# Weaving the MLA projection into the stick-breaking and MLA attention pipelines

## The reference

```
p = rmsnorm(x) @ w_in                      # 1024 -> 3*512 (q, k, v) + 384 + 256 + 32
o_sb  = stick-breaking attention, 8 heads of 64:
        z = q k^T / 8; A = exp(log_sigmoid(z) + sum over s<j<t of log_sigmoid(-z)), strictly causal; A v
q     = rmsnorm(c_q)  @ w_uq  -> 8 heads of 64 + 32 (the 32 get a rotary embedding)
k, v  = rmsnorm(c_kv) @ w_ukv -> 8 heads of 64 + 64, plus one rotary key of 32 shared by the heads
o_mla = softmax(q k^T / sqrt(96), causal) v
x = x + concat(rmsnorm(o_sb), rmsnorm(o_mla)) @ w_out
x = x + (silu(gate) * val) @ w_down,  gate, val = causal depthwise conv of rmsnorm(x) @ w_up
return rmsnorm(x)
```

## Time and profile before

| | |
|---|---|
| median of 2 runs | 3560.66 us (3554.89 to 3566.42) |
| the profiled execution's own time | 3548.83 us |
| its span on the slowest core (core 7) | 3546.7 us |
| spans of the 8 cores | 3519.6 to 3546.7 us, granted TensorE clock 0.940 to 0.947 of full speed |
| PE busy | 2507.5 us, 71% |
| ACT busy | 2076.0 us, 59% |
| DVE busy | 1425.7 us, 40% |
| POOL busy | 882.0 us, 25% |

### The profile page before, as it was taken

One profiled execution on the slowest core, in us unless ns is written; L12 is line 12 of the kernel. 1 busy time (PEld: TensorE's weight loads), 2 busy tenths in 40 slices (PEclk: granted clock), 3 DMA queues, 4 the chain that ended last, 5 costly groups with the idle time before them and its releaser, 6 DMA issues.

```text
span 3546.7 us, 57426 instructions; the slowest of 8 cores (3519.6 to 3546.7 us)
## 1 busy us (share of the span) xinstructions
PE 2507.5 (71%) x15344; PEld 1186.8 (33%) x15344; DVE 1425.7 (40%) x3146; ACT 2076.0 (59%) x4420; POOL 882.0 (25%) x1477
## 2 busy tenths in 40 slices
PE   4876666667656878788838766666676568787877
PEld 2432333234322333333324333232343233333333
DVE  3432222230314566666544322222303145666675
ACT  2458888867653444444234588888676544444442
POOL 2012222232332222222220122222323322222221
PEclk9999999999988999999969999999999889999999
DMA  5100000000039656565451000000000396566563
GB/s 112 48 14 1 1 1 1 1 1 1 1 78 136 90 95 85 95 92 82 60 120 48 13 1 1 1 1 1 1 1 1 75 142 99 88 91 92 87 86 63
DMA packets 211365, 178.48 MB, mean 50 GB/s; under 512 B 6000, under 2 KB 187248, under 8 KB 211056
## 3 DMA queue, kind: packets, MB, share of 16 engines
q0 software_dynamic: 195072, 119.29, 26.4%
q1 hardware_dynamic: 15984, 55.53, 4.8%
HBM read 277.30 MB, written 16.78 MB: 83 GB/s over the span
## 4 chain that ended last, share of the span: by engine, by line
PE 40%; ACT 22%; DVE 14%; issue 14%; POOL 5%; DMA 4%; ACTq 1%; another core or an unknown queue 1%; DVEq 1%; POOLq 0%; SPq 0%
PE pb L1027 9%; ACT arena L649 7%; PE pb L895 4%; ACT arena L795 4%; DVE arena L923 4%; PE pb L897 4%; DVE arena L926 4%; PE pb L634 3%; ACT arena L614 3%; PE pb L988 3%; PE pb L785 3%; PE pb L433 2%; PE pb L595 2%; ACT arena L913 2%; PE pb L636 2%
## 5 line engine op out<-in xcount | busy, mean ns | idle before, releaser
L641 DVE TENSOR_TENSOR arena<-arena 128x512 bf16<-128x512 bf16 (+3 forms) x576 | 226.7, 400 | 783.9 <-PE pb L595 447.6
L634 PE MATMUL pb<-arena,cbf_sb 128*128 128x512 bf16 (+3 forms) x640 | 222.2, 347 | 367.8 <-ACT arena L649 148.3
L895 PE MATMUL pb<-arena 128*128 128x512 bf16 x1408 | 346.7, 391 | 166.7 <-DVE arena L926 80.4
L616 ACT ACTIVATE arena<-arena 128x512 bf16<-128x512 f32 (+3 forms) x640 | 362.0, 566 | 108.7 <-POOL arena L652 24.2
L595 PE MATMUL pb<-arena 128*128 128x512 bf16 (+3 forms) x1280 | 411.3, 350 | 11.7 <-issue 4.3
L795 ACT ACTIVATE arena<-pb 128x512 bf16<-128x512 f32 (+3 forms) x640 | 314.7, 531 | 100.1 <-PE pb L822 65.1
L1027 PE MATMUL pb<-arena 128*128 128x512 bf16 x1408 | 324.6, 394 | 59.3 <-ACT arena L954 29.5
L913 ACT ACTIVATE arena<-pb,cw_sb 128x512 f32<-128x512 f32 x352 | 268.6, 775 | 155.1 <-PE pb L897 154.8
L614 ACT ACTIVATE arena<-pb 128x512 f32<-128x512 f32 (+3 forms) x640 | 336.4, 526 | 2.3 <-PE pb L595 1.9
L897 PE MATMUL pb<-arena 128*128 128x512 bf16 x1408 | 335.9, 382 | 0.0
L649 ACT ACTIVATE arena<-pb 128x512 bf16<-128x512 f32 (+3 forms) x640 | 329.8, 516 | 5.2 <-PE pb L595 3.5
(11 more groups left out here) (127 smaller groups left out, 3772.7 us busy)
## 6 DMA issues: line engine op xcount, KB each, us to landing
arena<-w_up POOLq DMA_DIRECT2D x176, 512.0 KB, 6.7
arena<-x SPq DMA_DIRECT2D x64, 512.0 KB, 4.4
out<-arena SPq DMA_DIRECT2D x32, 512.0 KB, 2.9
arena<-w_down POOLq DMA_DIRECT2D x22, 512.0 KB, 42.5
arena<-w_in POOLq DMA_DIRECT2D x16, 552.0 KB, 24.1
arena<-w_out POOLq DMA_DIRECT2D x16, 256.0 KB, 19.9
arena<-w_uq POOLq DMA_DIRECT2D x6, 192.0 KB, 5.4
arena<-g_mix SPq DMA_DIRECT2D x2, 512.0 KB, 5.5
```

The lines of the kernel that those rows point to most:

```text
L616: op('act', lambda e: e.activation(out=sp_sb[es_][:, 0:n], in_=e_sb[es_][:, 0:n], func=AF.Ln, bias=1.0), reads=[('e', es_)], writes=[('sp' ...
L634: e.matmul(banks[cbk][:, 0:n], lhsT=ntri, rhs=sp_sb[ss_][:, 0:n], start=True, stop=False)
L895: e.matmul(banks[bg][:], lhsT=wup[ws][:, kc, 0:128], rhs=h2T[:, kc, :], start=(kc == 0), stop=(kc == 7))
```

## The change

A second set of Q, K and V arrays is added (`QTm2`, `KTm2`, `Vm2`, "bufB"). Group 0's projection writes into it while SB runs, and group 1's projection writes into the old arrays ("bufA") while group 0's attention reads bufB. The projection is now a generator with 48 micro-steps (A, B, C for each block), of which `weave` issues one after every 6th step of the SB pipeline and after every 3rd of the first MLA attention. Its three banks come from the outputs of the attention: SB now uses banks 4 and 5 for every head, with the projection on 6 and 7; MLA uses 2, 3 and 4 for every head, with the projection on 5, 6 and 7. The barrier between SB and MLA goes. The tiles `qtm`, `ktm` and all of `Vm2` are filled by POOL before the first SB item; the fill of `Vs_flat` with ones stands once, between SB and the first MLA attention.

```diff
+def weave(main_gen, side_gen, every):
+    k = 0
+    for _ in main_gen:
+        k += 1
+        if side_gen is not None and k % every == 0:
+            next(side_gen, None)
+    if side_gen is not None:
+        for _ in side_gen:
+            pass
...
+            QTm2 = A3.take([128, 4, S], BF16)
+            KTm2 = A3.take([128, 4, S], BF16)
+            Vm2_flat = A3.take([128, NB * 260], BF16)
...
-                ob0 = 4 if h % 2 == 0 else 6
+                ob0 = 4
...
-            run_pipeline(sb_items, [(0, sb_s0), (1, sb_s1), (2, sb_s2), (3, sb_s3), (4, sb_s4)])
-            S_.barrier()
...
-                run_pipeline(list(range(NB)), [(0, mp_A), (1, mp_B), (2, mp_C)])
...
+                for tb in range(NB):
+                    step_A(tb)
+                    yield
+                    step_B(tb)
+                    yield
+                    step_C(tb)
+                    yield
...
-                    ob0 = 2 if h % 2 == 0 else 5
+                    ob0 = 2
...
+            for qs_ in range(2):
+                op('pool', lambda e, qs_=qs_: e.memset(qtm[qs_]..., 0.0), writes=[('qtm', qs_)])
+                op('pool', lambda e, qs_=qs_: e.memset(ktm[qs_]..., 0.0), writes=[('ktm', qs_)])
+            op('pool', lambda e: e.memset(Vm2_flat, 1.0), writes=[('Vb', tb) for tb in range(NB)])
+            n_micro = 3 * NB
+            weave(pipeline_gen(sb_items, [(0, sb_s0), (1, sb_s1), (2, sb_s2), (3, sb_s3), (4, sb_s4)]),
+                  mla_proj_gen(0, bufB, 6, 7, 6), max(1, len(sb_items) // (n_micro + 2)))
+            op('pool', lambda e: e.memset(Vs_flat, 1.0), writes=[('V', tb) for tb in range(NB)])
+            items0, stages0 = mla_attn_stages(0, bufB)
+            weave(pipeline_gen(items0, stages0), mla_proj_gen(1, bufA, 5, 6, 7), max(1, len(items0) // (n_micro + 2)))
+            items1, stages1 = mla_attn_stages(1, bufA)
+            run_pipeline(items1, stages1)
```

More of the change, by code:

```diff
@@ L194, in run_pipeline, with pipeline_gen @@
                 fn(items[i])
+def pipeline_gen(items, stages):
+    n = len(items)
+    maxlag = max(l for l, _ in stages)
+    for t in range(n + maxlag):
+        for lag, fn in stages:
+            i = t - lag
+            if 0 <= i < n:
+                fn(items[i])
+        yield
[8 more added lines that the diff above has]
+            pass
 class Arena:
@@ L684, in sb_s4, with mla_proj_gen, step_A @@
                              reads=[bk(bi)], pwrites=[('o', i)])
-            run_pipeline(sb_items, [(0, sb_s0), (1, sb_s1), (2, sb_s2), (3, sb_s3), (4, sb_s4)])
-            S_.barrier()
[L689 to L695, removed]
             MQ = 7
             n_mb = (NB + MQ - 1) // MQ
[L698 to L708, removed]
+            bufA = dict(QT=QT, KT=KT, V=Vs[:, :, 0:260].rearrange("p a (h d) -> p a h d", h=4),
+                        qk=lambda hl: ('QT', hl), kk=lambda hl: ('KT', hl // 2), vk=lambda tb: ('V', tb))
+            bufB = dict(QT=QTm2, KT=KTm2, V=Vm2,
+                        qk=lambda hl: ('QTb', hl), kk=lambda hl: ('KTb', hl), vk=lambda tb: ('Vb', tb))
+            def mla_proj_gen(g, bufs, bq, bkv, bt):
+                QTd, KTd, Vd = bufs['QT'], bufs['KT'], bufs['V']
+                def step_A(tb):
                     def mmq(e):
@@ L748, in mp_B, with step_C @@
                            reads=['kro'], pwrites=[kk_])
-                    op('dve', lambda e: e.tensor_copy(Vm[:, tb, :, 0:64], kvv[:, :, 64:128]), reads=[bk(bkv)], pwrites=[('V', tb)])
-                    S_.wtag(qk_, (g, tb))
-                def mp_C(tb, g=g):
+                    op('dve', lambda e: e.tensor_copy(Vd[:, tb, :, 0:64], kvv[:, :, 64:128]), reads=[bk(bkv)], pwrites=[bufs['vk'](tb)])
+                def step_C(tb):
                     qs = tb % 2
[L754 to L758, removed]
+                    qk_, kk_ = ('qtm', qs), ('ktm', qs)
+                    ptr = banks[bt][:].bitcast(BF16)
                     def trqk(e):
@@ L765, in trqk, with mla_attn_stages @@
                         return ins
[L766 to L770, removed]
-                run_pipeline(list(range(NB)), [(0, mp_A), (1, mp_B), (2, mp_C)])
-                if P3_MODE == 'proj':
-                    S_.enabled = False
+                    op('pe', trqk, reads=[qk_, kk_, 'cbf'], writes=[bk(bt)])
+                    evac(QTd[:, :, tb * 128:(tb + 1) * 128], ptr[:, 0:512].rearrange("p (a b) -> p a b", a=4),
+                         reads=[bk(bt)], pwrites=sorted(set(bufs['qk'](hl) for hl in range(4))))
+                    evac(KTd[:, :, tb * 128:(tb + 1) * 128], ptr[:, 512:1024].rearrange("p (a b) -> p a b", a=4),
+                         reads=[bk(bt)], pwrites=sorted(set(bufs['kk'](hl) for hl in range(4))))
+                for tb in range(NB):
[4 more added lines that the diff above has]
+                    step_C(tb)
+                    yield
+            def mla_attn_stages(g, bufs):
+                QTd, KTd, Vd = bufs['QT'], bufs['KT'], bufs['V']
+                base = mpc[0]
                 m_items = []
```

37 lines of the change are left out of this document (19 added, 18 removed).

## The result

The changed kernel took **1.0141** times the time of the one before (95% interval 1.0110 to 1.0172): about 3603 us against 3553 us, 50 us more. The forecast was 3552 us, in a range of 3480 to 3600; it was added to 3560.66 us, the median of two runs, which lies 7 us above the 3553 us. The profiled execution took 3596.8 us, its span 3595.3 us on core 3.

A forecast was written before the change was run, and what follows sets the result against it. It took ACT to bound SB, and a ring through two score banks the first MLA attention. Per sequence 5.4 + 26 - 38.7 + 36 - 41.9 + 9 = -4.2 us, twice -8.4: 3552 us, range 3480 to 3600.

The forecast's parts named there:

- Parts 1 and 4: Start of SB: POOL's fills, +5.4 us; SB to MLA: a projection stage goes, a fill stays, -38.7 us; per sequence.
- Part 2: Group 0's projection inside SB: ACT's three copies and one evac per block, plus waiting, +26 us per sequence.
- Part 3: One pair of output banks in SB: zeroing waits for both evacs, costing nothing, or up to 0.7 us per head change.
- Part 5: Group 1's projection inside the first MLA attention: 16 blocks at 2.25 us each, +36 us per sequence.
- w: Cost per block of weaving the projection into the first MLA attention: 2.25 us, own range 1.4 to 2.66.
- Part 6: First to second MLA attention: a 42.5 us projection stage goes, zeroing waits 0.6 us more, -41.9 us per sequence.
- Part 7: One set of MLA output banks: zeroing waits 1.5 us at 3 head changes in each group, +9 us per sequence.
- step C stands in PE's queue: First MLA attention: transposes wait for DVE's and POOL's step B, delaying scores and ACT; 3594 us, chance 0.14.
- It hides: First MLA attention: gaps take the woven work whole, at no cost per block; 3480 us, chance 0.18.
- The lock between DVE and GpSimd: Step B: two-input DVE and SBUF-reading GpSimd instructions lock each other out; little weight, 0.3 us per operation, 3650 us.
- the second rival: The rival "step C stands in PE's queue" in the first MLA attention: 3594 us, chance 0.14.

The follow-up runs named there:

- e2_attn_only: Changed kernel with group 0's projection not woven into SB but standing alone before the first MLA attention: 1.0160 of the kernel before, 3603.0 us.
- e4_evac_dve: Changed kernel with both copies of the transposes out of PSUM on DVE, none on ACT: 0.9910 of the kernel before, 3529.8 us.
- e8_filler: Changed kernel plus a 256-column zero-weight matmul behind each product with V of the first MLA attention: no ratio came out.
- e3_kfirst: Changed kernel with POOL's four rotary key copies issued in step A, ahead of ACT's copy: 1.0027 of the kernel before, 3567.2 us.
- e13_kfirst_evac: Changed kernel with POOL's rotary copies issued in step A and both transpose copies on DVE: 0.9856 of the kernel before, 3500.4 us.
- e16_filler512: Changed kernel plus a 512-column zero-weight matmul behind each product with V of the first MLA attention: 1.0094 of the kernel before.
- e6_alt_banks: Changed kernel with the second MLA attention's output banks alternating again between two sets: 1.0078 of the kernel before.
- e9_all_dve: Changed kernel with all projection work of ACT and POOL in steps B and C on DVE: 0.9740 of the kernel before, 3456.0 us.
- e5_kdve: Changed kernel with the rotary key written by one DVE copy in place of POOL's four: no ratio, lowest run 3564.2 us.

## Why the prediction was wrong

**Parts 1 and 4, the start of SB and the handover: right.** Forecast +5.4 and -38.7 us; measured +5.3 (`e2_attn_only`) and -38.8.

**Part 2, the projection inside SB: right in kind, 4.6 us too small.** ACT's own share was right: 22.6 us more busy (forecast 22.7). The term that was too small is the wait before the evac: I had 0.49 + 0.2 us for evac and wait, ACT's idle time there is 0.34 us, and by `e4_evac_dve` the two together cost 0.91 to 0.96 us: (0.22 to 0.27) x 16 = 3.5 to 4.3 us of the 4.6.

**Part 3, one pair of banks in SB: right.** `e2_attn_only` has the single pair, and from the first to the last product with V of SB it takes 506.1 us in the mean, where the kernel before takes 506.3.

**Part 5, the projection inside the first attention: this step failed.** I put w at 2.25 us a block and held 2.66 for its upper end, "if nothing overlaps". From a0, 166.4 - (144.8 - 41.9) - 4.5 = 59.0 us over 16 blocks: w = **3.7 us**, over the bound. The bound was no bound: work put into a ring of in-order engines can cost more than its length, because what queues behind it waits too. The sum of A, B and C looked at PE's and ACT's queues only and left out what POOL's four copies hold up. It shows most in the term for step C: 0.9 to 1.0 us for the transposes, a semaphore step and the evac, where ACT stood 20.9 / 16 = 1.3 us before the evac and then gave it its 0.5. And the sum took PE's durations from stages with a clock of 0.92 to 0.95 as if they would stay.

The 23.0 us divide about so, by estimates. The clock, from `e8_filler`: 13 us gross for 0.78 to 0.93. The order of POOL's copies, from `e3_kfirst`: 17.7 us, of which its own rise of the clock by 0.11 accounts for about 10 at the slope of 94 us, so some 8 directly. Together 21. But the two are not independent, and the slope is only a correlation. The windows would give the clock more: of the 15.5 us between the two stages shown, PE's busy time alone makes 12.7 (111.91 to 99.23). Which share is whose stays open. What the runs do show is the order of the two: taking waits away brought the clock up each time (`e3_kfirst` 0.886, `e4_evac_dve` 0.902, `e13_kfirst_evac` 0.936) and the time with it, while a full clock from fillers (`e16_filler512`, 0.976) left a0 at 160.4 us, the fillers' own price included. So the waits come first, and the lower clock adds to what they cost. No run changed the spacing of the micro-steps or the order of A, B and C among the items, which might remove the same waits.

**Part 6, from the first to the second attention: right**, the stage of 42.5 us went (what stands against it is part 5's).

**Part 7, the changes of heads: right in size.** 1.50 us at the zeroing where I had 1.5. a1 rose by 5.9 us, not 4.5, while the clock fell from 0.954 to 0.917, and `e6_alt_banks` took 7.5 off.

**The rival "step C stands in PE's queue"** had the right price (w = 3.55) by the wrong road: the transposes waited 0.3 us for step B. The queue that mattered was POOL's. Its 3594 us lacked parts 2 and 7's misses. **"It hides"** was far off with this placing of the work, but `e9_all_dve`, with ACT and POOL out of it, comes to w = 0.9 us by the same formula.

**The lock between DVE and GpSimd** was weighed by rows in which POOL ran only copies, and there it doesn't show. Beside POOL's masks, which read two arrays, it does (the first operation of step B's six and the next one on DVE, then POOL):

```profile
838.38 0.38 DVE L749 TENSOR_TENSOR arena<-arena 128x64 f32<-128x64 f32 x1 [5.04 <-ACT arena L744]
838.68 0.21 DVE L750 TENSOR_TENSOR arena<-arena 128x64 f32<-128x64 f32 x1
```

```profile
838.25 0.43 POOL L812 TENSOR_TENSOR arena<-arena,cbf_sb 128x128 bf16<-128x128 bf16 x1 [3.33 <-ACT arena L809]
839.15 1.23 POOL L756 COPY arena<-arena 128x32 bf16<-128x32 bf16 x4 [0.48 <-ACT arena L747]
```

Of the 3072 such operations of the eight cores, those with POOL idle beside them took 0.22 us in the mean, those that overlap a copy 0.23, and the 317 that overlap a mask 0.38. That is 20 operations a sequence and some 3 us of DVE, where the rival priced 1.8 us in every block; DVE has the time, and PE's transposes waited 0.3 us for it. `e5_kdve`, which took the copies from POOL, changed nothing that `e3_kfirst` had not.

**The range** ended at 3600 because the second rival was its end; w above it was considered only with a lock (3650 us), and the clock was in no case.

## What to carry to other kernels

Work that is woven into a pipeline should go to the engine that is idle there, not stay where it was while it ran alone: the same weave gave 1.0141 with ACT's and POOL's share left in place and 0.9740 with it on DVE (0.9635 with the output banks and the fills mended too). For each inserted instruction ask what it waits for and what stands behind it in its queue; an instruction of 0.2 us that waits for another engine costs the wait of all behind it, so the sum of lengths is no upper bound. And where PE's work gets gaps, price PE at both clock levels.

## What was not expected of the hardware

The granted clock moved within one stage between its two levels, and of the two windows shown PE was busy 57% in the one at full clock and 76% in the one at 0.66, since the same work lasts longer there: a high busy share is no sign of a high clock. A DVE multiplication that overlaps a mask on POOL took 0.38 us instead of 0.22, one beside POOL's copies 0.23. Adding 160 matmuls of 256 zero columns raised the clock from 0.78 to 0.93 and made the stretch a0 8.6 us shorter. POOL's fill costs 0.84 ns an element (6.92 us for 8192), and fills stood on the path at both ends of SB; filling only the columns that are read took 5.4 or 6.1 us off a handover.
